# Input projection in 512-column matmuls, its halves copied by ScalarE and added by GpSimd or VectorE

## What is computed

```python
h = rms_norm(x, pre_mix_g)
z = h @ w_in                                   # [256, 2048] @ [2048, 7296]
za, zb, zc = jnp.split(z, [NA_IN_COLS, NA_IN_COLS + RW_IN_COLS], axis=-1)
ya = neighbourhood_attention(*split3(za), na_rpb)      # 8 heads of 64
yb = rwkv7_mixer(zb, ...)     # token shift, then a recurrence, 12 heads, two directions
yc = retention_mixer(*split4(zc))                      # 6 heads of 128
x = x + rms_norm(concat(ya, yb, yc) @ w_out, post_mix_g)
h = rms_norm(x, pre_mlp_g)
x = x + rms_norm(square(relu(h @ w_up)) @ w_down, post_mlp_g)
```

## Time and profile before

| | us |
|---|---|
| median of 3 runs | 1355.17 (1351.14 to 1357.56) |
| span of the profiled execution | 1348.4 |
| dense stage, depths 0 to 336 | 19.6 to 143.7 |
| recurrence, depths 336 to 736 | 143.7 to 433 |
| hand-over, depths 736 to 760 | 433 to 443.9 |
| attention and retention, depths 760 to 912 | 443.9 to 530.5 |
| output projection and MLP | 530.5 to the end |

### The profile page before, as it was taken

How to read it: one execution, slowest core, us unless ns; L and a number is a source line. 1 busy time by engine, 2 the same in 40 slices (tenths; PEclk the granted TensorE clock), 3 DMA queues, 4 the chain that set the end, 5 groups by cost and what they waited for, 6 DMA issues and landing times.

```text
span 1348.4 us, 25311 instructions
## 1 busy us (share of the span) xinstructions
PE 1302.8 (97%) x10465; PEld 1142.9 (85%) x10465; DVE 841.8 (62%) x1185; ACT 646.5 (48%) x980; POOL 305.8 (23%) x243
## 2 busy tenths in 40 slices
PE   6999999999999899998999999999999999999996
PEld 5999888888899888877888888888888888888885
DVE  5566788789876986547555555555555545555455
ACT  5465654466434446447444444444444444444443
POOL 0011323233305121000455554444430000000000
PEclk9999999999999999998999999999999999999999
DMA  8666433232348334764766666666666666666663
GB/s 256 183 171 176 121 97 96 80 95 81 107 113 206 104 110 126 261 222 123 222 192 191 191 190 189 189 191 191 192 188 192 196 192 194 194 192 195 192 195 117
DMA packets 285750, 226.43 MB, mean 168 GB/s; under 512 B 15236, under 2 KB 263300, under 8 KB 284740
## 3 DMA queue, kind: packets, MB, share of 16 engines
q1 hardware_dynamic: 285168, 223.57, 56.4%
q0 software_dynamic: 240, 1.18, 0.3%
q10 hardware_dynamic: 228, 0.07, 0.0%
HBM read 222.69 MB, written 2.10 MB: 167 GB/s over the span
## 4 chain that ended last, share of the span: by engine, by line
PE 84%; DVE 8%; ACT 4%; issue 2%; DMA 1%; ACTq 0%; DVEq 0%
PE psum L2070 31%; PE psum L1717 17%; PE psum L1718 9%; PE psum L1706 7%; PE psum L1707 6%; PE psum L1708 6%; DVE w_lo L768 2%; PE psum L1836 1%; ACT w_hi L1321 1%; PE psum L1849 1%; DMA raw<-in_w_out 1%; PE psum L1773 1%; PE psum L1878 1%; PE psum L2125 0%; PE psum L1912 0%
## 5 line engine op out<-in xcount | busy, mean ns | idle before, releaser
L768 DVE TENSOR_TENSOR w_lo<-raw,w_hi 128x1024 fp32r<-128x1024 f32 x394 | 497.8, 1266 | 401.5 <-ACT w_hi L1321 400.6
L1321 ACT ACTIVATE w_hi<-raw 128x1024 fp32r<-128x1024 f32 x394 | 418.6, 1066 | 460.6 <-PE psum L2070 213.5
L1717 PE MATMUL psum<-act_both,w_hi 128*128 128x512 f32 x1024 | 355.6, 392 | 0.0
L2070 PE MATMUL psum<-w_hi,act_both 128*128 128x512 f32 x1216 | 327.4, 390 | 4.5 <-DVE act_both L1274 2.7
L1718 PE MATMUL psum<-act_both,w_lo 128*128 128x256 f32 x1024 | 286.7, 280 | 0.0
L1706 PE MATMUL psum<-act_both,w_hi 128*128 128x256 f32 x912 | 271.4, 298 | 7.5 <-DVE w_lo L768 6.0
L2070 PEld LDWEIGHTS psum<-w_hi,act_both 128*128 128x128 f32 x1216 | 227.7, 188 | 53.4 <-DVE act_both L1274 3.1
L1707 PE MATMUL psum<-act_both,w_hi 128*128 128x256 f32 x912 | 257.9, 283 | 0.0
L1708 PE MATMUL psum<-act_both,w_lo 128*128 128x256 f32 x912 | 257.6, 282 | 0.0
L1717 PEld LDWEIGHTS psum<-act_both,w_hi 128*128 128x128 f32 x1024 | 191.5, 187 | 42.3 <-DVE w_lo L768 0.2
L1718 PEld LDWEIGHTS psum<-act_both,w_lo 128*128 128x128 f32 x1024 | 193.5, 189 | 0.0
(11 more groups left out here) (234 smaller groups left out, 1084.7 us busy)
## 6 DMA issues: line engine op xcount, KB each, us to landing
raw<-in_w_up SPq DMA_DIRECT2D x128, 512.0 KB, 4.1
raw<-in_w_down SPq DMA_DIRECT2D x128, 512.0 KB, 4.5
raw<-in_w_in SPq DMA_DIRECT2D x114, 512.0 KB, 4.3
raw<-in_w_out SPq DMA_DIRECT2D x32, 512.0 KB, 4.5
arena<-in_x SPq DMA_DIRECT2D x2, 1024.0 KB, 6.1
arena<-in_na_rpb SPq DMA_DIRECT2D x16, 128.0 KB, 4.4
arena<-in_x SPq DMA_DIRECT2D x1, 2048.0 KB, 10.9
out_x<-arena SPq DMA_DIRECT2D x4, 512.0 KB, 2.7
```

Of the source, the lines that this page charges most:

```text
L768: dve.tensor_tensor(by_half(h, low(h)), by_pair(h, raw[:, h % RAW]), by_half(h, high(h)).bitcast(F32), ALU.subtract).then_inc(s["lo_half"], 1)
L1321: act.activation(by_half(h, high(h)), by_pair(h, raw[:, h % RAW]), ACT.Copy).then_inc(s["hi_half"], 1)
L1717: pe.matmul(bank[b].rearrange("p (a t) -> p a t", a=2), wh, act_both[:, :, kt], start=kt == 0, stop=False)
L2070: last = pe.matmul(bank[4 * t + 2 * j + b], lhs[:, tokens], w[:, b * 512:(b + 1) * 512], start=start, stop=stop)
```

## The change

TensorE now does a depth in two matmuls: the high weights meet both halves of the activation in one of 512 columns, which fills a whole bank (high by high in the left half, high by low in the right), and the low weights add 256 columns to the left half. The MLP's first product is already written so; its function is now used for both. A tile thus takes a bank by itself, tiles alternate between banks 6 and 7, and two halves have to be added.

- For tiles 0 to 44 (`POOL_TILES` = 45) ScalarE copies the left half to its place and the right half to one small buffer `rest`, and GpSimd adds the two. For tiles 45 to 56 ScalarE copies only the right half, and VectorE adds it to the left half straight out of PSUM.
- There is one `rest`: ScalarE's copy for tile n waits until tile n-1 is added. TensorE's first matmul of tile n waits until tile n-2 has been copied (up to tile 44) or added (from 45 on); before, it waited for a pair of tiles that ended at least 16 depths earlier.
- The scaled copy of an RW tile (`scale_z`) now reads `zpad` after GpSimd's sum, one tile at a time.
- In VectorE's gap the order is now add, `lo`, `shift`; before it was `shift`, `lo`. GpSimd now has gap calls.
- The mask of the key products is kept once per direction (it makes room for `rest`) and read with its halves swapped where needed; the products themselves are the same in number and size.

```diff
-HI_LAG, LO_LAG, DRAIN_LAG, SHIFT_LAG = 2, 5, 2, 6
+HI_LAG, LO_LAG, REST_LAG, SUM_LAG, SHIFT_LAG = 2, 5, 2, 4, 7
...
+        POOL_TILES = next(n for n in range(W_IN_T) if due(KT * (n + 1) + SUM_LAG) >=
+                          DENSE_GAPS + RW_CT * TURN_GAPS + TAIL_GAPS)
...
+            def gap():                                   # GpSimd
+                while at["sum"] < POOL_TILES and KT * (at["sum"] + 1) + SUM_LAG <= DONE[at["gap"]]:
+                    n = at["sum"]
+                    pool.wait_ge(s["most_out"], n + 1)
+                    pool.wait_ge(s["rest_out"], n + 1)
+                    pool.tensor_tensor(place_of(n), place_of(n), rest[:], ALU.add).then_inc(s["bank_free"], 1)
...
+            def add_rest(n):                             # VectorE
+                place_free(dve, n)
+                dve.wait_ge(s["rest_out"], n + 1)
+                dve.tensor_tensor(place_of(n), bank[6 + n % 2][:, 0:T], rest[:], ALU.add).then_inc(s["bank_free"], 1)
...
+            def take_rest(n):                            # ScalarE
+                act.wait_ge(s["gemm_half"], 2 * (n + 1))
+                if n < POOL_TILES:
+                    place_free(act, n)
+                    act.activation(place_of(n), bank[6 + n % 2][:, 0:T], ACT.Copy).then_inc(s["most_out"], 1)
+                if n:
+                    act.wait_ge(s["bank_free"], n)
+                act.activation(rest[:], bank[6 + n % 2][:, T:2 * T], ACT.Copy).then_inc(s["rest_out"], 1)
+            def scale_z(n):
+                act.wait_ge(s["bank_free"], n + 1)
+                act.activation(z_of(ct), zpad[:, n // 2 % 2, n % 2, 1:T + 1], ACT.Copy,
+                               scale=small[:, 64 + ct:65 + ct]).then_inc(s["z_scaled"], 1)
...
-                    if kt == 0 and first and q >= 2:     # TensorE
-                        pe.wait_ge(s["bank_free"], q - 1)
-                    depth(bank[6 + q % 2][:, 0:T] if first else bank[6 + q % 2][:, T:2 * T], x // HALF_KT, kt)
+                    if kt == 0 and n >= 2:
+                        pe.wait_ge(s["rest_out" if n - 2 < POOL_TILES else "bank_free"], n - 1)
+                    depth(6 + n % 2, x // HALF_KT, kt)
```

More of the change, by code:

```diff
@@ L205, in layer @@
         spare_hi, spare_lo = spare[:, 0], spare[:, 1]
+        rest = sb("rest", [P, T])
         psum = ctx.enter_context(nc.psum_tensor("psum", [P, 8, 512], F32))
@@ L476, in backwards, with halves_swapped @@
                            ap=steps[:-1] + [[-last, count]])
+        def halves_swapped(mask):
+            steps = [list(pair) for pair in mask.ap]
+            stride, count = steps[-2]
+            return bass.AP(tensor=mask.tensor, offset=mask.offset + stride * (count - 1),
+                           ap=steps[:-2] + [[-stride, count], steps[-1]])
         def spare_slot(h):
@@ L672, in products @@
                 steps[0]()
+                gap()
                 run(early[0])
@@ L676, in products @@
                     steps[n]()
+                    gap()
                     run(early[n])
             def level(t, p, n, steps, between, behind):
-                run(steps)
+                run(steps[:1])
+                gap()
                 run(between)
+                run(steps[1:])
+                gap()
                 run(behind)
@@ L692, in chunk @@
                 return decay_state if n in (1, 2) else nothing, nothing, nothing
-            stage_a(nothing, feed, tilde, products, level, chunk, STARTS)
+            stage_a(gap, feed, tilde, products, level, chunk, STARTS)
+            assert at["sum"] == POOL_TILES
             pool.wait_ge(s["bias_in"], 16 * ROWS * ROWS)
@@ L789, in shift, with add_until @@
                 last.then_inc(s["pad_free"], 1)
-            at = {"gap": 0, "lo": 1, "shift": 0}
+            def add_rest(n):
+                place_free(dve, n)
+                dve.wait_ge(s["rest_out"], n + 1)
+                dve.tensor_tensor(place_of(n), bank[6 + n % 2][:, 0:T], rest[:], ALU.add).then_inc(s["bank_free"], 1)
+            at = {"gap": 0, "lo": 1, "sum": POOL_TILES, "shift": 0}
+            def add_until(depth):
+                while at["sum"] < W_IN_T and KT * (at["sum"] + 1) <= depth:
+                    add_rest(at["sum"])
+                    at["sum"] += 1
             def gap():
                 done = DONE[at["gap"]]
+                add_until(done - SUM_LAG)
+                while at["lo"] < OUT_H + 2 and HALF_KT * (at["lo"] - SPLIT + 1) + LO_LAG <= reached(at["gap"]):
+                    lo(at["lo"])
+                    at["lo"] += 1
                 while at["shift"] < RW_GROUPS and KT * (group_tiles(at["shift"])[-1] + 1) + SHIFT_LAG <= done:
@@ L798, in gap @@
                     at["shift"] += 1
-                while at["lo"] < OUT_H + 2 and HALF_KT * (at["lo"] - SPLIT + 1) + LO_LAG <= reached(at["gap"]):
-                    lo(at["lo"])
-                    at["lo"] += 1
                 at["gap"] += 1
@@ L1196, in _ @@
                 turn(i)
-            assert at["lo"] == OUT_H + 2 and at["gap"] == len(DONE) - 1
+            add_until(DEPTHS)
+            assert at["lo"] == OUT_H + 2 and at["sum"] == W_IN_T and at["gap"] == len(DONE) - 1
             step[0] = base + NA_T // 3
@@ L1357, in _ @@
-            at = {"gap": 0, "hi": 1, "drain": 0}
-            def drain_until(depth):
-                while at["drain"] < GROUPS and KT * (group_tiles(at["drain"])[-1] + 1) <= depth:
-                    if at["drain"] < RW_GROUPS:
-                        to_zs(at["drain"])
-                    else:
-                        to_nr(at["drain"])
-                    at["drain"] += 1
-            def drain_rest():
-                drain_until(DEPTHS)
+            def take_rest(n):
[6 more added lines that the diff above has]
+                act.activation(rest[:], bank[6 + n % 2][:, T:2 * T], ACT.Copy).then_inc(s["rest_out"], 1)
@@ new lines, in scale_z, with rest_until @@
+            def scale_z(n):
+                ct = RW_ORDER[n]
+                act.wait_ge(s["bank_free"], n + 1)
+                act.activation(z_of(ct), zpad[:, n // 2 % 2, n % 2, 1:T + 1], ACT.Copy,
+                               scale=small[:, 64 + ct:65 + ct]).then_inc(s["z_scaled"], 1)
+            at = {"gap": 0, "hi": 1, "rest": 0, "scaled": 0}
+            def rest_until(depth):
+                while at["rest"] < W_IN_T and KT * (at["rest"] + 1) <= depth:
+                    take_rest(at["rest"])
+                    at["rest"] += 1
@@ L1376, in gap @@
                     at["hi"] += 1
+                while at["scaled"] < RW_T and KT * (at["scaled"] + 1) + SUM_LAG <= done:
+                    scale_z(at["scaled"])
+                    at["scaled"] += 1
                 at["gap"] += 1
@@ L1587, in _ @@
                 turn(i)
-            drain_rest()
-            assert at["hi"] == OUT_H + 2 and at["drain"] == GROUPS and at["gap"] == len(DONE) - 1
+            rest_until(DEPTHS)
+            assert at["hi"] == OUT_H + 2 and at["rest"] == W_IN_T and at["gap"] == len(DONE) - 1
             gate_heads(RET_CT - 2, RET_CT)
```

105 lines of the change are left out of this document (42 added, 63 removed).

## The result

The changed kernel takes 1367.27 us (median of 4 runs, 1366.41 to 1371.95) against 1356.06 us (4 runs, 1351.14 to 1357.56) for the kernel before: ratio 1.0107, interval 1.0077 to 1.0137. It is slower, where I had forecast no change: 11 us above the 1356.2 us that I gave, and 0.3 us beyond the range of 1345 to 1367. A later set of runs (experiment 9) has it at 1.0128, 1.0105 to 1.0151.

What follows compares the result with a forecast made beforehand. TensorE's pace was taken to bound the kernel up to depth 760, alternating with VectorE in attention. Terms -12.5 + 2.8 + 5.5 + 2.5 + 2.1 + 0.6 = +1.0 us gave a 1349.4 span, median 1356.2; range 1345 to 1367.

Steps and rivals of the forecast that it cites:

- The pace of the pair: Input projection: a depth as two matmuls takes 0.3463 us in place of 0.360, gaining 12.5 us over 912 depths.
- Depths 0 to 224 hidden: Early dense stage: ScalarE's extra copying, 0.46 us a tile, is covered by 1.3 us of room and costs 0.
- The hand-over: Between recurrence and attention: TensorE stalls 3.2 us at depth 752 for VectorE's sum of tile 45; cost 2.5 us.
- the clock's fall: Rival: a 3.2 us stall could lower TensorE's clock, losing 1.8 us, for 1358.0 us; chance 0.04.
- Late dense stage: Depths 224 to 288: copies cost 1.9 us and 0.9 of gain is lost; 2.8 us, between 0 and 6.
- Recurrence: Depths 336 to 736: unrealised gain 1.2, ScalarE's copies 2.4, VectorE slowed beside GpSimd's sums 1.9; 5.5 us in all.
- Attention: Attention and retention: ten more VectorE sums ahead of low parts cost 2.1 us, against a gain of 2.1.
- End: Last tile copied and added where one copy stood, with the previous sum ahead of the last heads: 0.6 us.
- The sum's last step: Total: the 6.8 us by which the runs' median exceeds the profiled span, added to 1349.4 us.
- The helpers swallow it: Faster rival: copies and sums outside the hand-over and the end fit in idle time; 1345.8 us, chance 0.18.
- The ring: Slower rival: in attention ScalarE's copy and VectorE's sum await each other through `rest`; 9.0 us for 2.1, 1363.1 us, chance 0.20.
- The pair no faster: Rival: weight loads eat the two-matmul gain, so nothing of 12.5 us comes; 1366.6 us, chance 0.05.

Runs made afterwards that it cites:

- experiment 9: The changed kernel run again unedited, against the kernel before: 1373.05 us, ratio 1.0128.
- 1: Changed kernel with ScalarE's copy of tile 45 ahead of the second root and VectorE's addition of it ahead of query scaling and normalisation: 1368.98 us, ratio 1.0116.
- experiment 3: Changed kernel with tile 45's copy and addition moved early and GpSimd's bias additions put ahead of its last sum: 1363.88 us, ratio 1.0084.
- experiment 2: Changed kernel with GpSimd's eight bias additions put ahead of its last sum (tile 44) instead of behind it: 1363.23 us, ratio 1.0088.
- 11: Kernel before, with GpSimd's eight bias additions held until depth 727 is done: 1358.75 us, ratio 1.0031.
- experiment 6: The kernel of experiment 3 with three 256-column matmuls again in 855 of 912 depths: 1363.77 us, ratio 1.0078.
- 8: Kernel before, with only the mask read with its halves swapped in place of two masks: 1351.19 us, ratio 0.9997.
- 10: The kernel of experiment 3, but GpSimd only waits for the copies of tiles 0 to 44 and frees the bank, adding nothing: 1354.99 us, ratio 1.0018.

## Why the prediction was wrong, by its steps

*The pace of the pair* was right: 0.3475 against 0.3463. *Depths 0 to 224 hidden*: right; between depths 8 and 216 TensorE gained 2.6 and 2.7 us (1.9 in experiments 1 and 3), 2.8 was the whole of it. *The mask*: right, 0.

The sizes of the misses: from depth 8 to 911 my terms and the gain come to +0.5 us, and the two profiles have 14.6 and 17.6. Of the 14 to 17 us between, the hand-over is 7.8 and 7.0 (measured 10.0 and 9.2, forecast 2.2), the dense stage 2.7 and 4.1 (forecast -1.7), the recurrence 2.2 and 3.4 (forecast 0), attention 1.5 and 2.6 (forecast 0).

*The hand-over* is the step that failed. "Here stands the one new wait that I can place", at depth 752 for tile 45: place and releaser were right, and the term of 2.5 (2.2 net of 24 faster depths) measured 10.0 and 9.2. I took VectorE's chain at its old length and did not ask what else had moved. GpSimd's last sum waits for ScalarE until 430, the bias additions behind it came to lie on the chain, and four of VectorE's instructions took 6.6 times as long. With them away (experiment 2) the wait is 3.58. And I priced the clock's fall at 1.8 us with a chance of 0.04 ("a stall of 3.2 us could do that too"): it came, cost 2.4 in eight depths, and came again in 1, 2 and 11 behind waits of 3.16, 3.58 and 2.12 us. It belonged in the term itself. So experiment 2, with the chain at its old length, still has 5.1 us and not 2.5: the whole wait counts, where I had let 0.7 of 3.2 be absorbed, and 1.5 of the clock comes on top.

*Late dense stage*, taken at 2.8, of it 1.9 for the copies: with the matmul's gain taken away, copies and sums cost 5.1 in the whole stage (experiment 6), of which one fall of the clock is about 1 (an estimate from the dense stages of 9 and 2 against those of the changed kernel, 1 and 3). The larger part of what the sums cost is GpSimd's order, 2.7, which the prediction did not look at. It put GpSimd's sums at nothing in the 2.8 (its bound of 6 had them waited for), and gave their appearance as what would make it wrong.

*Recurrence*, 5.5 for 5.5: 2.2 and 3.4 longer, 3.5 with the clock alike. Copies and sums cost 4.7 by experiment 6 and about 3.3 without the fall of the clock by which its profile has more than that of the kernel before (an estimate, at the 1.4 us of kernels 8 and 11), where I had 2.4 + 1.9 = 4.3. The term that was mis-sized is the gain not realised: 1.2 by the share of gaps with a wait; the pair gives 1.3 there of 5.1 (experiments 6, 9, 1 and 2), so 3.8 are lost. TensorE's waits grow from 9.4 to 14.6 us; the longest, 2.2 us for ScalarE's L1497, was 0.4 before.

*Attention*: 0 net forecast; 1.5 with the clock up in both profiles, 2.6 in the second one, in which it fell for 3.4 us, and 3.2 in experiment 3 with the clock up. TensorE waits 2.0 us more for low parts there (7.4, was 5.4), so the likely cause is VectorE's ten more sums ahead of them; no experiment takes these away, and it stays open. *End*, 0.6: the output projection begins 2.0 us behind depth 911 in both kernels, so nothing.

*The sum's last step.* I carried 6.8 us from the span of the profile to the median of the runs. Some of it is likely the two paces of the MLP told below: the profile was of the shorter kind, and the median run, of which no trace is kept, may be of the longer. That the median of the changed kernel came within 0.3 us of my range, whose upper end was reckoned for a pair without any gain, is luck.

*Rivals.* "The helpers swallow it" falls: even with the hand-over mended they don't. The ring did not close: in attention VectorE waits for ScalarE's copy in 2 places, 2.3 us in all, ScalarE nowhere for VectorE's sum, and TensorE for neither; the stage would have had to be 7 us longer and is 1.5 to 2.6. "The pair no faster" falls with the pace.

## What to carry to other kernels

When an engine's program gets new waits, follow what stands behind the last of them: work that ran ahead in free time is moved to where the wait ends, and may then lie beside someone's critical chain. Before a gain on the busiest engine is counted in full, ask in which gaps it is waited for by others; in a stage where a chain of small steps sets the pace, about a quarter came through here (1.3 of 5.1 us). Before the stages of two profiles are compared, compare their granted clock. A buffer's release belongs ahead of a long chain in every program that takes part in it, or the chain becomes part of the release.

## What the runs showed of the hardware

Beside GpSimd's 512-column additions, 1.6 us each, small instructions of VectorE suffer most: four 128x64 scalings take 0.49 us alone and 3.25 beside them, 0.8 each in place of 0.12; a 128x1024 subtraction 1.22 and 2.1. The reduction L1080, beside GpSimd's next products (443.87 to 445.27), keeps its 0.41. The Trainium skill (SBUF — State Buffer, "Who interferes with whom") says that scalings, which can run in a mode with both port pairs, and instructions with two SBUF inputs can be blocked for a whole instruction of GpSimd, and that reductions never are. The trace agrees in which of the three suffer. For the sums in the recurrence I had an estimate of 4.3 us by that rule beside my 1.9; the runs show 3.8 with the clock alike (3 less 10), nearer to the former. TensorE's granted clock fell to 0.50 at each wait of 7.3, 3.6, 3.2 and 2.1 us in the hand-over: in this order at 446.4 us (inside the wait), 450.1 (1.0 us behind its end), 448.7 (inside) and 443.9 (1.3 us behind). In experiments 3 to 8 and 10, without a wait there, it stayed at 1.00 through the hand-over. It also fell for 3.4 us where no such wait stood, as at 250.3 in the kernel before.

The MLP's first (up) product has two paces, whatever the kernel. Windows over the same 280 us, first of the kernel before, then of the kernel with the mask alone:

```profile
700.00:980.00 280.00, 280.00 (x1617) 246.91 (x1616) 145.69 (x127) 119.82 (x127) 139.90 (x75) 1.00 0.66 190
```

```profile
700.00:980.00 280.00, 280.00 (x1587) 242.83 (x1586) 141.97 (x124) 117.42 (x125) 140.02 (x74) 1.00 0.65 186
```

The same instructions at a granted clock of 1.00 in both, no wait, and 1617 matmuls against 1587: 0.346 and 0.353 us a depth (280 over half the count). From the end of the output projection to that of the up product it is 364.5 to 366 us in five of the profiles and 371 to 372 in the eight others, the two of the changed kernel among them. That is most of the 6 to 8 us by which the lower and the higher runs of a kernel lie apart (the down product takes 351.5 us in ten profiles and 353.1 in three), and it is why medians of few runs hide what the starts of the depths show. Its cause is open.
